# Turning the differential heads' queries and keys after the local heads, half on DVE and half on POOL

## The reference, cut to what matters

```python
qc = apply_rope(rms_norm(qc.reshape(B, S, 2 * C_HEADS, HEAD_DIM), qn_c[l]), cos, sin)
kc = apply_rope(rms_norm(kc.reshape(B, S, 2 * C_HEADS, HEAD_DIM), kn_c[l]), cos, sin)
vc = vc.reshape(B, S, C_HEADS, 2 * HEAD_DIM)
out_c = diff_attention(qc, kc, vc, lam)      # softmax(q0 k0) - lam * softmax(q1 k1), times v
...
merged = (g[:, :, 0] * (out_a @ w_oa[l]) + g[:, :, 1] * (out_b @ w_ob[l]) + g[:, :, 2] * (out_c @ w_oc[l]))
x = x + merged @ w_out[l]
```

## Time and profile before

| | us |
|---|---|
| median of 3 runs (lowest, highest) | 1126.22 (1123.49, 1126.56) |
| the profiled execution's own time | 1125.78 |
| its span, from the first to the last instruction | 1124.0 |
| mean granted TensorE clock | 0.991 |
| PE busy | 1073.8 (96%) |
| DVE busy | 724.5 (64%) |
| ACT busy | 540.0 (48%) |
| POOL busy | 59.5 (5%) |

### The profile page before, as it was taken

How to read it: one execution, slowest core, us unless ns; L and a number is a source line. 1 busy time by engine, 2 the same in 40 slices (tenths; PEclk the granted TensorE clock), 3 DMA queues, 4 the chain that set the end, 5 groups by cost and what they waited for, 6 DMA issues and landing times.

```text
span 1124.0 us, 14634 instructions
## 1 busy us (share of the span) xinstructions
PE 1073.8 (96%) x4942; PEld 866.4 (77%) x4942; DVE 724.5 (64%) x1193; ACT 540.0 (48%) x828; POOL 59.5 (5%) x64
## 2 busy tenths in 40 slices
PE   4999999999999999999999999889799999999998
PEld 3777678888887778788888778767577877888887
DVE  2865775554557987755555577987848676555553
ACT  3564454444444556644344473645347535444442
POOL 5003000000000200000000000002400000000000
PEclk9999999999999999999999999999899999999999
DMA  9454256555555543566565543543244455555553
GB/s 250 125 169 131 77 164 190 187 186 187 188 186 172 169 147 127 158 190 189 184 191 188 176 150 113 169 132 113 76 133 135 144 169 169 187 187 187 187 187 112
DMA packets 133599, 182.04 MB, mean 162 GB/s; under 512 B 11446, under 2 KB 80322, under 8 KB 133490
## 3 DMA queue, kind: packets, MB, share of 16 engines
q1 hardware_dynamic: 132266, 178.40, 50.2%
q0 software_dynamic: 1056, 2.57, 1.1%
q10 hardware_dynamic: 232, 0.49, 0.1%
HBM read 180.36 MB, written 1.05 MB: 161 GB/s over the span
## 4 chain that ended last, share of the span: by engine, by line
PE 77%; DVE 13%; ACT 5%; issue 2%; DMA 2%; SPq 1%; POOL 0%; DVEq 0%; ACTq 0%; POOLq 0%
PE ps L1793 15%; PE ps L1804 14%; PE ps L1796 14%; PE ps L1814 7%; PE ps L1815 6%; PE ps L1819 6%; DVE wlo L1032 4%; PE ps L1778 2%; PE ps L1780 2%; PE ps L1779 2%; ACT whi L571 1%; PE ps L1884 1%; DMA raw<-in_a_w_in 1%; PE ps L1867 1%; PE ps L2006 1%
## 5 line engine op out<-in xcount | busy, mean ns | idle before, releaser
L1032 DVE TENSOR_TENSOR wlo<-raw,whi 128x1024 fp32r<-128x1024 f32 x338 | 407.1, 1236 | 151.8 <-ACT whi L571 151.3
L571 ACT ACTIVATE whi<-raw 128x1024 fp32r<-128x1024 f32 x338 | 342.3, 1052 | 117.3 <-DMA raw<-in_ffn_w_out 29.0
L1793 PE MATMUL ps<-whi,ath 128*128 128x512 f32 (+1 forms) x896 | 360.6, 403 | 9.1 <-DVE atl L1046 5.5
L1796 PE MATMUL ps<-whi,atl 128*128 128x512 f32 (+1 forms) x896 | 351.9, 393 | 0.0
L1804 PE MATMUL ps<-wlo,ath 128*128 128x512 f32 (+1 forms) x896 | 240.7, 390 | 3.3 <-DVE wlo L1032 3.3
L1793 PEld LDWEIGHTS ps<-whi,ath 128*128 128x128 f32 x896 | 170.4, 190 | 53.7 <-issue 11.6
L1804 PEld LDWEIGHTS ps<-wlo,ath 128*128 128x128 f32 x896 | 167.2, 188 | 40.1 <-DVE wlo L1032 5.4
L1796 PEld LDWEIGHTS ps<-whi,atl 128*128 128x128 f32 x896 | 170.7, 191 | 33.5 <-issue 0.5
L1814 PE MATMUL ps<-whi,brh 128*128 128x512 f32 x272 | 106.5, 392 | 0.5 <-issue 0.5
L1815 PE MATMUL ps<-whi,brl 128*128 128x512 f32 x272 | 105.9, 389 | 0.0
L1108 DVE TENSOR_TENSOR brl<-ps,brh 128x512 fp32r<-128x512 f32 x33 | 22.8, 692 | 95.2 <-ACT brh L617 95.2
(11 more groups left out here) (339 smaller groups left out, 1027.2 us busy)
## 6 DMA issues: line engine op xcount, KB each, us to landing
raw<-in_ffn_w_in SPq DMA_DIRECT2D x176, 256.0 KB, 2.9
raw<-in_ffn_w SPq DMA_DIRECT2D x132, 256.0 KB, 2.9
raw<-in_w_in SPq DMA_DIRECT2D x104, 256.0 KB, 2.9
raw<-in_ffn_w_out SPq DMA_DIRECT2D x88, 256.0 KB, 2.8
raw<-in_a_w_in SPq DMA_DIRECT2D x48, 256.0 KB, 3.3
raw<-in_b_w_in SPq DMA_DIRECT2D x48, 256.0 KB, 3.0
raw<-in_a_w_out SPq DMA_DIRECT2D x16, 256.0 KB, 2.8
raw<-in_b_w_out SPq DMA_DIRECT2D x16, 256.0 KB, 2.8
```

Source lines behind the costliest of these rows:

```text
L571: a_(unit_view(whi, slot, w), unit_view(raw, slot, w), ACT.Copy).then_inc(hi_ready, 1)
L1032: v_.tensor_tensor(unit_view(wlo, slot, w), unit_view(raw, slot, w), unit_view(whi, slot, w), ALU.subtract).then_inc(lo_ready, 1)
L1793: mm(ps[bk + t][:, 0:w], ath[:, k, t * P:(t + 1) * P], rh[:, kk, :], start=k == 0, stop=False)
L1796: mm(ps[bk + t][:, 0:w], atl[:, k, t * P:(t + 1) * P], rh[:, kk, :], start=False, stop=False)
```

## The change

The turning moves behind the last `w_prob` and is split. POOL does tile 1 alone, once `c_ssq` is 6 and `w_p` is 16 (all eight local heads weighed). DVE does tile 0 in a new function, `d_turn_angles`, in round 8 of its loop, behind that round's `feed` and ahead of round 9's `w_out(3)`. Its scratch is `hid` and `sil` in place of `C_z`. On ACT `gate_evac(23, 1)` goes ahead of `d_copy(0)` and `d_copy(1)`. PE's and SP's lists are as they were.

```diff
@@ POOL
             pool.wait_ge(evac_act, ACT_EVACS[18])
-            pool.wait_ge(sem("c_ssq"), 5)
+            pool.wait_ge(sem("c_ssq"), 6)
+            pool.wait_ge(sem("w_p"), 2 * WQ)
...
-            for t in range(NT):
-                y = C_pd[:, t, 0:1024].rearrange("p (h d) -> p h d", h=16)
...
+            y = C_pd[:, 1, 0:1024].rearrange("p (h d) -> p h d", h=16)
...
+            pool.wait_ge(sem("c_d_norms"), 1)
+            nc.gpsimd.tensor_tensor(y[:, 8:16, :], y[:, 8:16, :],
+                                    sm[:, 344:352].unsqueeze(2).to_broadcast([P, 8, HD]), ALU.mult)\
+                .then_inc(sem("c_d_ready"), 1)
@@ ACT
+            gate_evac(23, 1)
             d_copy(0)
             d_copy(1)
-            gate_evac(23, 1)
             feed(U_OA + 4)
@@ DVE
+            def d_turn_angles():
+
+                z = [half.rearrange("p (h d) -> p h d", h=8) for half in (hid_flat, sil_flat)]
+                y = C_pd[:, 0, 0:1024].rearrange("p (h d) -> p h d", h=16)
+                for kind in range(2):
+                    hs = slice(8 * kind, 8 * kind + 8)
+                    for lo in (0, HD // 2):
+                        hi = lo + HD // 2
+                        ins = v_.tensor_tensor(z[kind][:, :, lo:hi], y[:, hs, HD // 2 - lo:HD - lo],
+                                               C_T2[:, 2 + kind, 0, lo:hi].unsqueeze(1).to_broadcast([P, 8, HD // 2]), ALU.mult)
+                link(ins)
+                for kind in range(2):
+                    hs = slice(8 * kind, 8 * kind + 8)
+                    ins = v_.tensor_tensor(y[:, hs, :], y[:, hs, :],
+                                           C_T1[:, 2 + kind, 0, :].unsqueeze(1).to_broadcast([P, 8, HD]), ALU.mult)
+                link(ins)
+                for kind in range(2):
+                    hs = slice(8 * kind, 8 * kind + 8)
+                    ins = v_.tensor_tensor(y[:, hs, :], y[:, hs, :], z[kind], ALU.add)
+                link(ins)
+                v_.tensor_tensor(y[:, 8:16, :], y[:, 8:16, :],
+                                 sm[:, 328:336].unsqueeze(2).to_broadcast([P, 8, HD]), ALU.mult)\
+                    .then_inc(sem("c_d_ready"), 1)
+
...
+                if i == WQ:
+                    dve.wait_ge(sem("c_d_norms"), 1)
+                    d_turn_angles()
                 if i == 2:
                     c_sums(3, C_z, 320, 16)
```

More of the change, by code:

```diff
@@ L513, in _ @@
             pool.wait_ge(evac_act, ACT_EVACS[18])
-            pool.wait_ge(sem("c_ssq"), 5)
+            pool.wait_ge(sem("c_ssq"), 6)
+            pool.wait_ge(sem("w_p"), 2 * WQ)
             z = C_z.rearrange("p (h d) -> p h d", h=16)
-            d_steps = 0
-            for t in range(NT):
-                y = C_pd[:, t, 0:1024].rearrange("p (h d) -> p h d", h=16)
[L519 to L532, removed]
-                        .then_inc(sem("d_rot"), 1)
[L534 to L545, removed]
+            y = C_pd[:, 1, 0:1024].rearrange("p (h d) -> p h d", h=16)
[3 more added lines that the diff above has]
+                    hi = lo + HD // 2
+                    nc.gpsimd.tensor_tensor(
+                        z[:, hs, lo:hi], y[:, hs, HD // 2 - lo:HD - lo],
+                        C_T2[:, 2 + kind, 1, lo:hi].unsqueeze(1).to_broadcast([P, 8, HD // 2]), ALU.mult)\
+                        .then_inc(sem("d_rot"), 1)
@@ new lines, in _ @@
+            pool.wait_ge(sem("d_rot"), 4)
+            for kind in range(2):
+                hs = slice(8 * kind, 8 * kind + 8)
+                nc.gpsimd.tensor_tensor(y[:, hs, :], y[:, hs, :],
+                                        C_T1[:, 2 + kind, 1, :].unsqueeze(1).to_broadcast([P, 8, HD]), ALU.mult)\
+                    .then_inc(sem("d_rot"), 1)
+            pool.wait_ge(sem("d_rot"), 6)
+            nc.gpsimd.tensor_tensor(y, y, z, ALU.add).then_inc(sem("d_rot"), 1)
+            pool.wait_ge(sem("d_rot"), 7)
```

## The result

| | us |
|---|---|
| changed kernel, median of 8 runs (lowest, highest) | 1130.12 (1127.93, 1132.80) |
| kernel before, median of 8 runs | 1125.76 (1122.40, 1129.32) |
| ratio, 95% interval | 1.0043 (1.0024 to 1.0063) |
| its profiled execution, span | 1128.57, 1126.8 |

A forecast was written before the change was run, and what follows sets the result against it. PE, busy for 96% of the span, was taken to bound the kernel. The terms -11.7 + 10.1 + 3.7 + 4.1 gave +6.2 us on 1125.8, so 1132.0 us, range 1125.5 to 1136.5.

The forecast's parts named there:

- (1): Local heads 3 and 4: with POOL's work gone, PE's waits and the low clock behind them go, -11.7 us.
- (2): Behind the last `w_prob`: DVE and POOL exclude each other while turning, so PE goes on later, +10.1 us.
- (3): Behind PE's wait for the turning: the granted clock is low, +3.7 us, bounds 1.7 and 4.5.
- (4): Ahead of `d_scores(0)`: PE waits for ACT's copies, with a low clock behind, +4.1 us, bounds 2.1 and 6.4.
- Rival A: Turning behind the last `w_prob`: DVE and POOL work side by side, wait 3.4 us, 1121.6 us; chance 0.12.
- B: Behind the last `w_prob`: exclusion holds, but clock recovers quickly and order costs its least, +2.5, 1128.3 us; chance 0.18.
- C: Clock stays low from the first new wait to behind the second, +10.7, 1136.5 us; chance 0.10.
- D: Local heads: the next head, 5, takes part of the gain, 1 to 2 us more, 1133.5 us; chance 0.10.

The follow-up runs named there:

- spread kernel: Changed kernel, but DVE turns tile 0 in round 5, tile 1 in round 7, POOL none, ACT's order of before: 1115.87 us; with the change's ACT order 1120.49 us.
- single tiles: Two kernels, the changed kernel with only DVE's tile turned and with only POOL's tile turned: 1121.92 and 1124.90 us, one run each.

## Why the prediction was right, step by step

The terms of the profiled executions, each the shift of one PE instruction between before and after:

| step | forecast | measured | from |
|---|---|---|---|
| (1) heads 3 and 4 | -11.7 | -11.8 | head 5 at 797.11, was 809.66, less 0.74 that it was ahead already |
| (2) wait for the turning | +10.1 | +8.8 | transposes at 826.40, were 830.14 |
| (3) clock behind it | +3.7 | +2.9 | last products of unit 243 at 832.88, were 833.73 |
| (4) ACT's order | +4.1 | +2.3 | `d_scores(1)` at 854.93, was 853.49 |
| sum | +6.2 | +2.2 | |

The 0.74 us come from ahead of the stage (head 3's last products begin at 779.85, before at 780.59), so they are no part of the change: from 758 to 761 us the clock of before stood at 0.50 and that of the changed kernel at 1.00. With them the two profiled executions are 1.4 us apart at `d_scores(1)`. The other 1.4 of the 2.8 come from 907 to 911 us, far behind the change, where the clock fell in the changed kernel's execution and not in that of before (first the changed kernel, then before):

```profile
908.00:910.00 2.00, 2.00 (x10) 1.90 (x9) 0.50 (x2) 1.00 (x4) 0.00 (x0) 0.50 0.50 188
...
908.00:910.00 2.00, 2.00 (x10) 1.55 (x10) 1.97 (x6) 2.00 (x3) 0.00 (x0) 1.00 0.16 46
```

The medians are 4.4 apart. Of these the trace explains 2.2; where the other 2.2 arise, in executions without a trace, isn't shown. Terms (2) to (4) are together 3.9 us too large by the trace, and the forecast of the time missed by only 1.9. So its closeness is partly luck.

(1) was right to 0.1 us: the waits went, nothing came in their place, and the kernel without the turning shows the same.

(2) The mechanism was right, the size 1.3 us too large. I had counted each of POOL's instructions by its full duration in the profile, 8.7 us in all. They add 7.0 us to DVE's list, 0.2 us less for each of the eight. DVE's own part, 2.3 + 4.3 = 6.6 in the forecast, takes 7.0 by itself. The 15.3 us of the forecast were thus 14.0, and the 0.4 of `w_out(3)` came on top as written.

(3) 2.9 in place of 3.7. The row of a longer low clock behind a wait of 7.17 us was taken as nearest to one of 8.6, but the clock was back at 832.4, 6.0 us after PE resumed, not 8. The waits and their low clocks don't go by length: behind 6.3 us (DVE with both tiles) some 1.9 us were lost, behind 5.1 us (POOL's tile alone) 2.7, behind 14.0 us (POOL late) 2.1, and behind 8.7 us with ACT's order of before 2.4. In each of these traces the loss is about half of the time from PE's first transpose to the clock's return (3.8, 5.6, 4.3 and 5.0 us).

(4) The wait was 3.31 us, forecast 3.4, and 1.1 us of it were given back at `d_scores(1)`, forecast 1.0. The 1.7 us for the clock did not fall due in the profiled execution. They did in that of the spread kernel with this order, and there more than I gave (2.9), and in that with both tiles on DVE (1.6). The changed kernel's own runs are spread from 1127.9 to 1132.8, and the three slowest have the lowest mean clocks, 0.987 to 0.988, against 0.990 to 0.992 in the others. That the clock's fall behind this wait is what separates them fits, but these runs have no trace, so it isn't shown; stretches of low clock elsewhere, as the one at 907 us, would do the same.

Rival A (no exclusion, 1121.6) is refuted by the single tiles. B (1128.3: the clock recovers early, the order costs its least) comes near the profiled execution, +2.5 against +2.2, but its wait was 1.3 us too long and its clock 1.2 us too cheap, so that two errors cancel; the median lies between B and the forecast. C (the clock low from the first wait to behind the second) is refuted in this trace, as the clock was back at 832.4 and stayed at 1.00 behind the second wait. D (the next head takes part of the gain) falls, as head 5 had no wait.

The rule of the Trainium skill (SBUF — State Buffer, "SBUF: two separate sides"), that the shared port pair is locked for the whole instruction, led to the right mechanism. Measured here is a little less than the whole profiled duration: 7.0 of 8.7 us.

## What to carry to other kernels

Before giving half of an elementwise job to POOL, look at what DVE does in that time: where both read two tensors from SBUF, as here, the split cost nearly the sum, and DVE alone with both halves had PE wait less (6.3 against 8.6 us; the times of the two kernels are too close to tell apart). Moving a helper's work out of one stage only pays if the place it goes to has idle time and nobody waits for it; here DVE had 2.9 and 4.0 us idle a few rounds earlier, and the same work cost nothing there. And the order of two independent steps in one engine's list decides a wait when one of them waits for the engine that the other releases.

## What the runs showed of the hardware

An instruction of POOL with two SBUF inputs delays DVE's next by less than its profiled duration: in the changed kernel one product of 0.70 us comes between the two `wlo` and lengthens the pair from 2.35 to 2.88, by 0.53 us. The other way round, two `wlo` of 1.13 each lengthen POOL's four products to 4.61 us, though the first product began 0.25 us into the first `wlo`. Undisturbed they take 2.75, as in the second tile of the kernel in which POOL turns late:

```profile
822.82 2.75 POOL L524 TENSOR_TENSOR work<-work 128x256 f32<-128x256 f32 x4
```

Not every instruction of DVE is held up. Beside POOL's turning in the kernel before, a TENSOR_SCALAR from SBUF to SBUF is, though it reads one tensor: one takes 2.37 us that takes 0.17 in the changed kernel, and a pair takes 3.53 in place of 0.62. A SCALAR_TENSOR_TENSOR with an input in PSUM and a TENSOR_REDUCE are not; beside POOL, in the kernel before, they take what they take at 805 us without it (0.87 and 0.69):

```profile
782.05 0.86 DVE L1624 SCALAR_TENSOR_TENSOR work<-ps,sm,con 128x256 f32<-128x256 f32 x2
782.94 0.69 DVE L1628 TENSOR_REDUCE sm<-work 128x2 f32<-128x512 f32 x1
```

And the same wait of 3.3 us of PE left the granted clock at 1.00 in three traces (the changed kernel's and those of either tile alone) and let it fall to 0.50 in two others, at a price of 1.6 us (both tiles on DVE) and 2.9 us (the spread kernel with this order). So such a wait has several prices, and a median can mix them.
